# First loads on one DMA queue in order of use, and the first norm's sum of squares later, in a two-block fp32 transformer kernel

## What is computed

```python
xn = x * rsqrt(mean(x * x, axis=-1) + EPS) * norm_mix_g   # RMS norm over the 1024 features
proj = xn @ w_in                                          # first columns: sb_q, then sb_k, sb_v, ...
sb_q, sb_k, sb_v, g_q, ... = split(proj)
o_sb = stick_breaking_attention(sb_q, sb_k, sb_v)
...
```

## Time and profile before

| | before |
|---|---|
| median of 3 runs | 1911.25 us (1910.7 to 1913.84) |
| the profiled execution: time | 1911.94 us |
| its span, first to last instruction | 1910.1 us |
| PE busy | 1881.0 us (98%) |
| DVE, ACT, POOL busy | 920.4 us (48%), 754.4 us (39%), 771.2 us (40%) |
| mean granted TensorE clock | 1.000 |
| DMA moved | 223.96 MB, mean 117 GB/s |

### The profile page before, as it was taken

One profiled execution on the slowest core, in us unless ns is written; L12 is line 12 of the kernel. 1 busy time (PEld: TensorE's weight loads), 2 busy tenths in 40 slices (PEclk: granted clock), 3 DMA queues, 4 the chain that ended last, 5 costly groups with the idle time before them and its releaser, 6 DMA issues.

```text
span 1910.1 us, 24398 instructions
## 1 busy us (share of the span) xinstructions
PE 1881.0 (98%) x9272; PEld 1532.9 (80%) x9272; DVE 920.4 (48%) x1241; ACT 754.4 (39%) x945; POOL 771.2 (40%) x227
## 2 busy tenths in 40 slices
PE   9999999999999999989999999999999999999999
PEld 6877788878888887646788888888998778888887
DVE  6455525676505554875866236629664371101111
ACT  6455344343323345365532222244377452322221
POOL 3322323434344344301343444343495443344333
PEclk9999999999999999999999999999999999999999
DMA  5122212445435534102355255433321223233322
GB/s 215 56 89 67 67 56 92 161 177 200 137 116 197 201 110 157 66 1 102 141 198 177 92 190 189 149 105 100 111 68 68 88 89 104 73 100 108 110 72 94
DMA packets 46509, 223.96 MB, mean 117 GB/s; under 512 B 4944, under 2 KB 9296, under 8 KB 31840
## 3 DMA queue, kind: packets, MB, share of 16 engines
q1 hardware_dynamic: 32896, 173.87, 26.8%
q10 hardware_dynamic: 13536, 49.03, 6.7%
HBM read 220.75 MB, written 2.13 MB: 117 GB/s over the span
## 4 chain that ended last, share of the span: by engine, by line
PE 81%; DVE 6%; issue 5%; POOL 4%; ACT 2%; DMA 1%; SPq 0%; ACTq 0%; DVEq 0%; POOLq 0%
PE pairs L563 39%; PE pairs L591 19%; PE pairs L1127 4%; PE pairs L615 4%; PE pairs L582 2%; PE pairs L898 2%; PE pairs L905 2%; POOL wl L2270 2%; POOL arena L2028 2%; PE pairs L541 2%; PE pairs L412 1%; DMA raw<-in_w 1%; PE aux L1710 1%; DVE xl L509 1%; DVE arena L1474 1%
## 5 line engine op out<-in xcount | busy, mean ns | idle before, releaser
L2270 POOL TENSOR_TENSOR wl<-raw,wh 128x2048 fp32r<-128x2048 f32 (+2 forms) x169 | 696.4, 4121 | 1087.7 <-ACT wh L525 1087.7
L525 ACT ACTIVATE wh<-raw 128x2048 fp32r<-128x2048 f32 x171 | 326.7, 1911 | 296.6 <-PE pairs L591 209.0
L563 PE MATMUL pairs<-xh,wh 128*128 128x512 f32 x1120 | 436.2, 389 | 3.7 <-DVE aux L796 1.5
L563 PE MATMUL pairs<-xh,wl 128*128 128x512 f32 x1120 | 435.7, 389 | 0.0
L563 PE MATMUL pairs<-xl,wh 128*128 128x512 f32 x1120 | 435.7, 389 | 0.0
L563 PEld LDWEIGHTS pairs<-xh,wh 128*128 128x128 f32 x1120 | 210.3, 188 | 48.8 <-issue 2.1
L563 PEld LDWEIGHTS pairs<-xl,wh 128*128 128x128 f32 x1120 | 210.3, 188 | 43.6
L563 PEld LDWEIGHTS pairs<-xh,wl 128*128 128x128 f32 x1120 | 210.3, 188 | 43.3
L591 PE MATMUL pairs<-zl,wh 128*128 128x512 f32 x518 | 201.5, 389 | 0.0
L591 PE MATMUL pairs<-zh,wl 128*128 128x512 f32 x518 | 201.5, 389 | 0.0
L591 PE MATMUL pairs<-zh,wh 128*128 128x512 f32 x518 | 201.5, 389 | 0.0
(11 more groups left out here) (343 smaller groups left out, 3018.7 us busy)
## 6 DMA issues: line engine op xcount, KB each, us to landing
raw<-in_w SPq DMA_DIRECT2D x113, 1024.0 KB, 5.0
arena<-in_ada ACTq DMA_DIRECT2D x88, 512.0 KB, 5.4
raw<-in_w SPq DMA_DIRECT2D x48, 704.0 KB, 4.1
raw<-in_w SPq DMA_DIRECT2D x12, 512.0 KB, 3.6
arena<-in_ada SPq DMA_DIRECT2D x8, 512.0 KB, 5.7
arena<-mx_rows SPq DMA_DIRECT2D x16, 256.0 KB, 3.6
h<-in_xT SPq DMA_DIRECT2D x4, 512.0 KB, 9.2
outT<-h SPq DMA_DIRECT2D x8, 256.0 KB, 5.3
```

The costliest lines, as they stand in the source:

```text
L525: a.activation(wh[:, slot, :], raw[:, slot, :], ACT.Copy).then_inc(hi_done, 1)
L563: mm = p.matmul(pairs[:, 2 * slot + m, :], w[:, slot, at:at + P], src[part][:, k, :], start=(k == 0 and w is wh and part == 0), stop=(k == ...
L2270: g.tensor_tensor(wl[:, slot, 0:w], raw[:, slot, 0:w], wh[:, slot, 0:w].bitcast(F), ALU.subtract).then_inc(lo_done, 1)
```

## The change

It changes only the opening. (1) All first loads go through SP's queue, in the order of use: `par`, tile 0, weight quarter 0, tile 1, tiles 2 and 3, quarter 1, tiles 4 and 5, the second weight half, tiles 6 and 7; then chunk 1, constants, `cond_row` and the later chunks as before. (2) ACT makes the high part of chunk 0 in four quarters between the scaled tiles, and DVE the remainders likewise. (3) ACT makes two squares, then the high part of chunk 2, then the other six squares; the call at the head of `norm_act` is left out for this norm. (4) PE's `norm_sum_pe` stands after tile 4 of chunk 1, not after tile 1. (5) Four products of zeros in place of five. (6) `cond_row` and the constants share one semaphore, so waits on `consts` wait for both; other counts are adapted to the added increment of `half_lo` and `half_hi`.

```diff
+X_PARTS = [(0, 1), (1, 2), (2, 4), (4, 6), (6, 8)]
...
             def scaled(k):
-                a.wait_ge(x_in[k // 2], 16)
+                for i, (k0, _) in enumerate(X_PARTS):
+                    if k == k0:
+                        a.wait_ge(x_in[i], 16)
                 a.activation(zh[:, k, :], h[:, k, :], ACT.Copy, scale=pc("norm_mix", k)).then_inc(u_hi, 1)
 
-            for at, to, done in ((0, QW, half_in[0]), (QW, HW, quarter_in), (HW, 2 * HW, raw_full[0])):
-                a.dma_start(raw[:, 0, at:to], w2048[0:1, :, at:to].rearrange("a p n -> p (a n)")).then_inc(done, 16)
+            def quarter(i):
+                if i < 3:
+                    a.wait_ge((half_in[0], quarter_in, raw_full[0])[i], 16)
+                a.activation(wh[:, 0, i * QW:(i + 1) * QW], raw[:, 0, i * QW:(i + 1) * QW], ACT.Copy
+                             ).then_inc(half_hi if i < 3 else hi_done, 1)
...
             for k in range(KT):
+                if k == 2:
+                    hi_part(a, 2, 0)
                 if k >= 2:
                     a.wait_ge(sq_acc, k - 1)
                 a.activation(FSQ[k % 2], h[:, k, :], ACT.Square).then_inc(sq_done, 1)
...
             for k in range(KT):
-                if k < 2:
-                    at = slice(k * QW, (k + 1) * QW)
-                    v.wait_ge(half_hi, k + 1)
...
                 v.wait_ge(u_hi, k + 1)
                 v.scalar_tensor_tensor(zl[:, k, :], h[:, k, :], pc("norm_mix", k), zh[:, k, :].bitcast(F),
                                        ALU.mult, ALU.subtract).then_inc(u_ready, 1)
+                if k in (0, 2):
+                    quarter_low(k // 2)
+                if k == 4:
+                    quarter_low(2)
+                    quarter_low(3)
...
             ahead = C0[NORM_TO[name]] + (1 if n else 2)
-            hi_part(a, ahead, ahead % 2)
+            if n:
+                hi_part(a, ahead, ahead % 2)
...
-            for _ in range(5):
+            for _ in range(4):
                 p.matmul(pairs[:, 2, :], WARM[:, 0:P], WARM, start=True, stop=True)
             for c in range(2):
                 for k in range(KT):
-                    if c == 0 and k < 4:
+                    if c == 0 and k < 6:
                         p.wait_ge(half_lo, k // 2 + 1)
                     elif c and k < 4:
-                        p.wait_ge(half_lo, 3)
+                        p.wait_ge(half_lo, 4)
...
-                    if c == 1 and k == 1:
+                    if c == 1 and k == 4:
                         norm_sum_pe(p, "n_mix")
```

More of the change, by code:

```diff
@@ L131, in build @@
         consts, par_in = sem("consts"), sem("par_in")
-        x_in = [sem(f"x_in{i}") for i in range(4)]
+        x_in = [sem(f"x_in{i}") for i in range(len(X_PARTS))]
         ones_in = sem("ones_in")
@@ L271, in scaled @@
             def scaled(k):
-                a.wait_ge(x_in[k // 2], 16)
+                for i, (k0, _) in enumerate(X_PARTS):
+                    if k == k0:
+                        a.wait_ge(x_in[i], 16)
                 a.activation(zh[:, k, :], h[:, k, :], ACT.Copy, scale=pc("norm_mix", k)).then_inc(u_hi, 1)
-            for at, to, done in ((0, QW, half_in[0]), (QW, HW, quarter_in), (HW, 2 * HW, raw_full[0])):
-                a.dma_start(raw[:, 0, at:to], w2048[0:1, :, at:to].rearrange("a p n -> p (a n)")).then_inc(done, 16)
+            def quarter(i):
[3 more added lines that the diff above has]
+                             ).then_inc(half_hi if i < 3 else hi_done, 1)
             a.preload_act_table_set("natural_log_exp_and_others")
             a.wait_ge(par_in, 16)
[L279 to L284, removed]
+            scaled(0)
+            quarter(0)
+            scaled(1)
+            scaled(2)
+            quarter(1)
+            scaled(3)
+            scaled(4)
+            quarter(2)
+            quarter(3)
+            for k in range(5, KT):
                 scaled(k)
@@ L547, in body @@
                 if in_halves:
-                    p.wait_ge(half_lo, 5)
+                    p.wait_ge(half_lo, 6)
                 else:
@@ L762, in body @@
                 a.wait_ge(hid_done, f + 1)
-                a.wait_ge(consts, 16)
+                a.wait_ge(consts, 32)
                 a.activation(zh[:, bass.ds(l, 1), :], HID[:, slot:slot + 1, :], ACT.Copy).then_inc(hid_hi, 1)
@@ L986, in sb_pe @@
             half_pe(p, 1)
-            p.wait_ge(consts, 16)
+            p.wait_ge(consts, 32)
             for u in range(SB_N):
@@ L1081, in out_lo @@
                 v.tensor_tensor(zl[:, pr, :], pv_of(pr), zh[:, pr, :].bitcast(F), ALU.subtract).then_inc(z_lo, 1)
-            v.wait_ge(consts, 16)
+            v.wait_ge(consts, 32)
             arguments(0)
@@ L2014, in ml_gpsimd @@
             g.wait_ge(m_utc, 2)
-            g.wait_ge(consts, 16)
+            g.wait_ge(consts, 32)
             for n in range(MN):
@@ L2200, in _, with x_load, w_load @@
         def _(sp):
+            def x_load(i):
+                k0, k1 = X_PARTS[i]
+                sp.dma_start(h[:, k0:k1, :], xT[:, k0 * T:k1 * T].rearrange("p (k t) -> p k t", t=T)
+                             ).then_inc(x_in[i], 16)
+            def w_load(at, to, done):
+                sp.dma_start(raw[:, 0, at:to], w2048[0:1, :, at:to].rearrange("a p n -> p (a n)")).then_inc(done, 16)
             sp.dma_start(par[:, :], par_d).then_inc(par_in, 16)
[L2203 to L2205 removed]
             x_load(0)
+            w_load(0, QW, half_in[0])
+            x_load(1)
+            x_load(2)
+            w_load(QW, HW, quarter_in)
+            x_load(3)
+            w_load(HW, 2 * HW, raw_full[0])
+            x_load(4)
             for stage, kind, _ in STAGES:
@@ L2215, in body @@
                     else:
[L2216 to L2219, removed]
+                        if c == 1:
                             sp.dma_start(raw[:, slot, 0:HW], w2048[c:c + 1, :, 0:HW].rearrange("a p n -> p (a n)")
@@ L2225, in body @@
                             sp.dma_start(cst[:, P:], cst_d[:, P:]).then_inc(consts, 16)
-                            sp.dma_start(cond_row[:, :], c_d.to_broadcast([P, D])).then_inc(cond_in, 16)
+                            sp.dma_start(cond_row[:, :], c_d.to_broadcast([P, D])).then_inc(consts, 16)
                         return
@@ L2289, in _ @@
             norm_act(a, "n_mix")
-            a.wait_ge(cond_in, 16)
+            a.wait_ge(consts, 32)
             a.activation(cond_row[:, :], cond_row[:, :], ACT.Silu).then_inc(cond_done, 1)
```

22 lines of the change are left out of this document (12 added, 10 removed).

## The result

| | before | changed |
|---|---|---|
| median of 10 runs | 1911.6 us | 1916.85 us (1913.84 to 1917.75) |
| ratio | | 1.0022 (1.0014 to 1.0030), or +4.2 us (+2.7 to +5.7) |
| profiled execution: time, span | 1911.94, 1910.1 us | 1916.03, 1914.2 us |
| mean granted TensorE clock | 1.000 | 0.997 |

The change makes the kernel slower by about 0.2%. The ratio compares the runs as a whole and not the two medians: the means are 1912.1 and 1916.4 us, which gives 1.0022, while the medians alone would give 1.0027 (+5.25 us). A second measurement beside the experiments gave 1.0020 (1.0011 to 1.0029).

A forecast was written before the change was run, and what follows sets the result against it. TensorE was taken to bound the opening, the norm chain having 1.66 us of slack. TensorE's path came 3.3 us earlier, the sum 3.6 later, chunk 3 +2.1: 1911.25 + 2.1 = 1913.3 us, range 1910.3 to 1916.0.

The forecast's parts named there:

- Loads: Opening DMA loads: bytes ahead of the last x tiles unchanged, last pair still landing at 13.3, tile 0 at 5.7.
- Start of TensorE: Opening, chunk 0: first real pass at 8.0, tile 2 at 10.8, TensorE's own path 3.3 us earlier.
- Squares: ACT in chunk 1: six squares wait behind chunk 2's load, landing at 21.4; sum starts 3.6 us later, at 28.7.
- What follows the sum: From the sum to chunk 3: the chain keeps its length, chunk 3 starts at 47.13 against 45.05, +2.1 us.
- rival of TensorE's own path: Opening: squares hidden, TensorE's path decides, chunk 3 starts at 41.7, -3.4 us or 1907.9; chance 0.06.
- One queue slower: Opening loads: SP's queue alone at 350 GB/s, chunk 2 landing at 24.5, +5.2 us or 1916.5; chance 0.08.
- Chunk 2 early: Chunk 2's load lands by 19.3, chunk 3 starts at 45.05 as before, 0.0 us or 1911.3; chance 0.12.
- the clock falls while PE stands: TensorE at the sum: clock drops during the wait, +3.6 us if only chunk 1's 18 passes, +15 at most; chance 0.03.

The follow-up runs named there:

- e1: Changed kernel with the high part of chunk 2 put back behind all eight squares; ratio to the kernel before 1.0006.
- e2: Kernel before with only the high part of chunk 2 moved between the second and third square; ratio to the kernel before 1.0034.
- e9: Changed kernel with the high part of chunk 2 before the seventh square in place of the third; ratio to the kernel before 1.0007.
- e10: Changed kernel with chunk 2's high part behind the squares, chunk 1's renormalizing late, two squares and additions between first tiles, sum after tile 2; ratio to before 0.9990.
- e5: Changed kernel with chunk 2's high part behind the squares, sum after tile 3, chunk 0's three pieces issued from ACT's queue; ratio to the kernel before 1.0002.
- e6: Changed kernel with the large constants and `cond_row` (1216 KB) issued behind chunk 2's load; ratio to the kernel before 1.0006, median 1914.15 us.
- e7: Changed kernel with three products of zeros on TensorE ahead of the sum over the partitions; ratio to the kernel before 1.0021.
- s3: Kernel before with three more products of zeros ahead of chunk 2, delaying TensorE 2.58 us while busy; ratio to the kernel before 1.0015.
- a1: Changed kernel measured once more, unaltered; ratio to the kernel before 1.0020, median 1915.65 us.

## Why the prediction was right

Its direction and its mechanism held; most terms of the opening were right to some tenths, and the total was undersized. The ratio puts the changed kernel at 1911.25 x 1.0022 = 1915.5 us, inside the range of 1910.3 to 1916.0 but near its end; the median of its runs, 1916.85, lies above it. The prediction called so small a difference the same as none. The measured one is clear of zero, and whether it is over the 0.2% to which the prediction gave 0.08 its interval (0.14 to 0.30%) leaves open. That the number fell within the range owes something to its width, since about half of the measured difference was not in the sum.

- *Loads.* Expected and measured landings: `par` 4.65 and 3.1, tile 0 5.7 and 4.0, quarter 0 6.4 and 6.1, the last tiles 13.3 and 13.3. `par` was early in every profile with one queue (2.2 to 2.3 us from issue to landing in nine, 3.7 to 4.0 in the four with two queues), but TensorE waits for quarter 0.
- *Start of TensorE.* 8.0 expected, 7.54 measured; tile 2 at 10.8 and 11.02; the sum's place in the order at 25.8 and 26.11.
- *Squares.* The wait of ACT for chunk 2 was the main step. 21.4 expected, 21.83 measured; last addition 28.55 and 28.92; sum 28.7 and 29.06; TensorE's wait 2.9 and 2.79. The load was issued 0.7 us later than before, at 14.02, because chunk 0's last remainder came later, and took 7.8 us in place of 8.1. e1, e2 and e9 show the cause: take the squares from behind the wait and 2.2 to 2.6 us of the loss are gone, make the move alone and it is all there, doubled (in e2 behind a wait for TensorE's last pass of chunk 0, the other condition of the same high part).
- *What follows the sum* is the term that was undersized. +2.1 expected, +2.65 measured: 0.36 from the later landing and sum, 0.15 to 0.2 from a slower start of Ln behind the sum's last pass on a falling clock (30.30 for 29.06, where it was 26.16 for 25.11).
- *The rival of TensorE's own path* stayed refuted for this kernel, and e10 shows what it takes to make it true. *One queue slower* is refuted by the load of chunk 2 itself, landed at 21.8 and not at 24.5, and by e5, which gains nothing with two. The prediction reads the 417 GB/s of the earlier trace rows as a rate of both queues; ACT's last piece had landed at 10.96, so from 12 to 14 us it was SP's queue alone. With both queues, from 8 to 10 us, the rate was 410. That speaks against this rival even more. *Chunk 2 early* stays open, as e6's profile did not bring it about.
- **The step that failed** is the rival "the clock falls while PE stands". I gave it 0.03 because the earlier trace rows show a wait of 2.8 us without a fall. It fell, after 2.79 us. Its price I had at +3.6 for 18 slow passes; in fact some 7 passes were slow and the norm chain covered them (e7: 0.1 us). The rule that the prediction took from the Trainium skill, "TensorE: Matmul & The Clock Gate", Part 1, that the throttled state is the default and activity releases it, agrees with this trace (0.50 from 30 to 32 us, behind the wait of 2.79). One wait in which the clock did not fall was no evidence for the next.
- *The term missing from the sum* is the clock in the untouched part. I took the profile of before, at a clock of 1.000, for the kernel's usual state, and it is not. In the pair of profiles that gave 1.45 us of the 4.1, and by what the executions of before show it is chance which of them has such a fall. How much of the measured 4.2 (2.7 to 5.7) stays behind the opening's 2.65 is open. On the chip of the first group the kernel before got to TensorE 0.4 to 0.6 us sooner (13.55 in s3, 13.72 in e2, for 14.11), which by estimate would make the opening's share about 3.1 there, if the changed kernel starts chunk 3 at the same time on that chip; the rest lies within the interval. Whether a shift changes how often the clock falls later could not be told.

## What to carry to other kernels

A high-priority piece of work moved up in a strictly ordered engine takes its waits along: before moving it, look when its input lands, and count what would stand behind it and who waits for that. A load that nobody waits for in a profile is not a load that is early. When a change is worth a few us, look at the granted clock of both profiles stage by stage first, since a fall of the clock at an untouched wait (here 1.7 us) is more than half as large as the effect of the change (2.65).

## What the runs showed of the hardware

- TensorE's clock fell to 1.2 GHz after waits of 2.79 us at 26 us and of 1.96 us at 802 us (changed kernel) and of 1.86 us at 26.5 us (e6), but not, in the profile of before, after 2.00 us at the place of the second, nor after 2.85 us at 834 us. The same wait can thus cost nothing or 1.7 us. A fall in front of another wait cost nothing (near 836 us in the changed kernel).
- The first DMA, 149.5 KB, landed 2.2 to 2.3 us after its issue in the nine profiles in which one queue starts alone, and 3.7 to 4.0 after it in the four in which a second queue starts beside it.
- A 1 MB load issued into a queue with the constants ahead of it (1216 KB) took 7.8 us in the changed kernel and 7.5 in a1, and 6.9 with them behind it in e6: taking 3 us worth of bytes away (at 417 GB/s) brought 0.6 to 0.9 us.
